# Sliding attention scores from 128 stacked rows: two full matmuls a block in place of three of 64 rows

## What is computed

```python
qb = q.reshape(b, nb, BLOCK, SWA_KV_HEADS, SWA_GROUP, SWA_HEAD_DIM)      # head size 64, blocks of 128 tokens
kk = jnp.concatenate([kp[:, :-1], kp[:, 1:]], axis=2)                    # the block before and the block itself
scores = jnp.einsum('bnqhgd,bnkhd->bnhgqk', qb, kk).astype(jnp.float32) * (SWA_HEAD_DIM ** -0.5)
scores = jnp.where(valid[None, :, None, None], scores + alibi, NEG)
probs = jax.nn.softmax(jnp.concatenate([scores, sink], axis=-1), axis=-1)[..., :-1]
out = jnp.einsum('bnhgqk,bnkhd->bnqhgd', probs.astype(v.dtype), vv)
```

## Time and profile before

| what | value |
|---|---|
| time, median of 3 runs | 2956.63 us (2955.93 to 2957.34) |
| span of the profiled execution, first to last instruction | 2956.8 us |
| PE busy | 2841.3 us, 96% of the span |
| DVE, ACT, POOL busy | 45%, 34%, 37% |
| mean granted TensorE clock | 0.975 |
| swa stages | about 160 to 410 us and 908 to 1160 us of the span |

### The profile page before, as it was taken

The page is one execution under the profiler, slowest core; times in us unless marked ns, Lnnn a source line. Parts: engine busy times, 40 slices in busy tenths (PEclk is TensorE's granted clock), DMA queues, the critical chain, the costliest instruction groups (busy, mean ns, idle before and its releaser), DMA issues.

```text
span 2956.8 us, 33732 instructions
## 1 busy us (share of the span) xinstructions
PE 2841.3 (96%) x13276; PEld 2324.0 (79%) x13276; DVE 1342.4 (45%) x1855; ACT 999.1 (34%) x1558; POOL 1092.7 (37%) x536
## 2 busy tenths in 40 slices
PE   7999999999999999999999999999999999999985
PEld 5888887778888888777777888788878888888774
DVE  6656545732365555474135445444344222222345
ACT  5234434522323343452333233323223232333221
POOL 3443341234443333222434333333434444444431
PEclk9999998999999999899999999999999999999997
DMA  5332231234433223113433222222323333336332
GB/s 158 105 102 72 72 113 37 55 100 139 139 93 121 72 68 117 42 42 96 137 123 85 72 72 75 75 72 68 97 86 112 110 114 107 114 107 214 110 111 93
DMA packets 307613, 288.11 MB, mean 97 GB/s; under 512 B 33152, under 2 KB 256000, under 8 KB 306944
## 3 DMA queue, kind: packets, MB, share of 16 engines
q1 hardware_dynamic: 300656, 263.93, 30.0%
q10 hardware_dynamic: 6800, 22.02, 1.9%
HBM read 259.66 MB, written 26.21 MB: 97 GB/s over the span
## 4 chain that ended last, share of the span: by engine, by line
PE 80%; DVE 13%; ACT 4%; issue 2%; POOL 1%; DMA 0%; DVEq 0%; SPq 0%; ACTq 0%
PE bank L813 23%; PE bank L815 22%; PE bank L814 22%; PE work L813 2%; DVE probs L1533 2%; PE work L814 1%; PE work L815 1%; PE o_bank L813 1%; PE work L1034 1%; PE o_bank L814 1%; PE o_bank L815 1%; DVE pt L1541 1%; DVE mixed L1109 1%; DVE mixed L1108 1%; POOL w_lo L804 1%
## 5 line engine op out<-in xcount | busy, mean ns | idle before, releaser
L804 POOL TENSOR_TENSOR w_lo<-w_raw,w_hi 128x1024 fp32r<-128x1024 f32 (+3 forms) x468 | 1004.0, 2148 | 1545.0 <-ACT w_hi L669 1544.8
L813 PE MATMUL bank<-act_in,w_hi 128*128 128x512 f32 x2664 | 1058.4, 397 | 38.4 <-DVEq L1194 24.7
L815 PE MATMUL bank<-act_in,w_lo 128*128 128x512 f32 x2664 | 1044.1, 392 | 0.0
L814 PE MATMUL bank<-act_in,w_hi 128*128 128x512 f32 x2664 | 1042.7, 391 | 0.0
L669 ACT ACTIVATE w_hi<-w_raw 128x1024 fp32r<-128x1024 f32 (+3 forms) x468 | 437.8, 937 | 1096.8 <-PE bank L815 700.3
L813 PEld LDWEIGHTS bank<-act_in,w_hi 128*128 128x128 f32 x2664 | 503.3, 189 | 149.4 <-POOL w_lo L804 18.3
L815 PEld LDWEIGHTS bank<-act_in,w_lo 128*128 128x128 f32 x2664 | 502.3, 189 | 108.2
L814 PEld LDWEIGHTS bank<-act_in,w_hi 128*128 128x128 f32 x2664 | 503.5, 189 | 99.3 <-issue 1.4
L813 PE MATMUL bank<-mixed,w_hi 128*128 128x512 f32 x768 | 303.0, 394 | 6.4 <-POOL w_lo L804 6.4
L814 PE MATMUL bank<-mixed,w_hi 128*128 128x512 f32 x768 | 301.7, 393 | 0.0
L815 PE MATMUL bank<-mixed,w_lo 128*128 128x512 f32 x768 | 301.0, 392 | 0.0
(11 more groups left out here) (230 smaller groups left out, 2897.7 us busy)
## 6 DMA issues: line engine op xcount, KB each, us to landing
w_raw<-in_w_in SPq DMA_DIRECT2D x512, 128.0 KB, 2.4
w_raw<-in_w_in SPq DMA_DIRECT2D x224, 256.0 KB, 2.9
w_raw<-in_w_out SPq DMA_DIRECT2D x64, 512.0 KB, 3.6
w_raw<-in_w_in SPq DMA_DIRECT2D x32, 512.0 KB, 3.7
w_raw<-in_w_out SPq DMA_DIRECT2D x64, 256.0 KB, 4.7
probs<-in_xT SPq DMA_DIRECT2D x32, 256.0 KB, 4.8
x_scr<-buf ACTq DMA_DIRECT2D x32, 256.0 KB, 2.2
probs<-x_scr SPq DMA_DIRECT2D x32, 256.0 KB, 4.9
```

What stands on the lines that cost most here:

```text
L804: nc.gpsimd.tensor_tensor(lo, raw, hi, ALU.subtract).then_inc(lo_ready, 1)
L813: pe.matmul(dst, lhs[0], rhs[0], start=start, stop=False, skip_group_check=skip)
L814: pe.matmul(dst, lhs[0], rhs[1], start=False, stop=False, skip_group_check=skip)
L815: return pe.matmul(dst, lhs[1], rhs[0], start=False, stop=stop, skip_group_check=skip)
```

## The change

The same query tile is held in another form. For each head e, `mixed[:, t, e]` now has all 128 partitions: the hi part of the head in its own 64 partitions and its lo part in the other 64. The keys get a plane pair for each e: `k_swa[:, e, 0]` has the keys' hi in both halves, `k_swa[:, e, 1]` has the keys' lo in the head's own half and zeros in the other. One matmul over 128 rows gives hi·hi + lo·hi, a second gives hi·lo, both with the same weights. The copies and subtractions on DVE are done by halves of 64 partitions, since a result has to go to the other half. `k_swa` has grown to 2048 columns and lies in another place, which the latents' DMA reads; so the keys are written in `swa_values`, behind the wait for that DMA.

```diff
-        k_swa = y_flat[:, 6144:7168].rearrange("p (s t) -> p s t", s=2)
+        k_swa = y_flat[:, 2048:4096].rearrange("p (e s t) -> p e s t", e=2, s=2)
...
-                    rows = slice(64 * e, 64 * e + 64)
...
-                        q = mixed[rows, t, :, i * P:(i + 1) * P]
-                        k = k_swa[rows, :, k0:k0 + w]
-                        ins = three(dst, (q[:, 0], q[:, 1]), (k[:, 0], k[:, 1]), True, True)
+                        q = mixed[:, t, e, i * P:(i + 1) * P]
+                        pe.matmul(dst, q, k_swa[:, e, 0, k0:k0 + w], start=True, stop=False)
+                        ins = pe.matmul(dst, q, k_swa[:, e, 1, k0:k0 + w], start=False, stop=True)
...
+            def head_rows(e):
+                return slice(64 * e, 64 * e + 64)
...
                     v.tensor_tensor(acc2[:, :], acc2[:, :], sq[:, :], ALU.add).then_inc(sum_in, 1)
-                    link(split(k_swa, tmp[:, 0, :]))
...
                 v.wait_ge(bank_free, tile_no[gi, m] + 1)
-                if m < 2:
-                    hi_lo = mixed[:, 2 * i + m] if kind == "swa" else (q_sb, k_sb[:, :, META:TM])[m]
-                    link(split(hi_lo, dst))
+                if kind == "swa":
+                    q = mixed[:, 2 * i + m]
+                    for e in range(2):
+                        ins = v.tensor_copy(q[head_rows(e), e, :], dst[head_rows(e), :])
+                    link(ins)
+                    for e in range(2):
+                        own, other = head_rows(e), head_rows(1 - e)
+                        ins = v.tensor_tensor(q[other, e, :], dst[own, :], q[own, e, :].bitcast(F32), ALU.subtract)
+                    link(ins)
+                elif m < 2:
+                    link(split((q_sb, k_sb[:, :, META:TM])[m], dst))
                 signal(tile_ready)
...
                     v.wait_ge(lat_saved, 16 * (l + 1))
+                    k = tmp[:, 0, :]
+                    for e in range(2):
+                        own, other = head_rows(e), head_rows(1 - e)
+                        v.memset(k_swa[other, e, 1, :].bitcast(F32), 0.0)
+                        v.tensor_copy(k_swa[other, e, 0, :], k[own, :])
+                        ins = v.tensor_copy(k_swa[own, e, 0, :], k[own, :])
+                    link(ins)
+                    for e in range(2):
+                        own = head_rows(e)
+                        v.tensor_tensor(k_swa[own, e, 1, :], k[own, :], k_swa[own, e, 0, :].bitcast(F32),
+                                        ALU.subtract)
```

## The result

The changed kernel takes **2972.27 us** (median of 4 runs, 2968.74 to 2977.13) against 2956.28 us before: a ratio of **1.0051, 95% interval 1.0037 to 1.0065**. Measured once more later, with more rounds, it was 1.0069 (1.0053 to 1.0084). It is slower, by 11 to 25 us. The profiled execution is the fastest of the four: its span is 2967.0 us, and the run's time 2968.74.

What follows compares the result with a forecast made beforehand. DVE with ACT was taken to bound the swa group ends, with PE waiting; 2956.8 less 19.5 gained on PE plus 34 lost gives 2971.3, forecast 2971 us, range 2955 to 2984.

Steps and rivals of the forecast that it cites:

- The bound: At the 8 swa group ends DVE with ACT is the bound; PE waits 0.4 us before the first head's transposes.
- The gain: PE's score blocks: 0.83 us a head, 19.5 us in sum; the 8 first heads bring nothing.
- a part for the form: PE's score blocks: leaving matmuls of 64 rows gives back 0.38 us a head.
- one for the number: PE's score blocks: four matmuls fewer a head give 0.45 us.
- The loss: DVE's added query splits at the 8 group ends, with standing behind POOL: 34 us in sum.
- A group end of the usual kind: Six group ends: 4.2 us more each, 2.3 of work and 1.9 behind POOL; 25.2 us.
- a layer's first group end: First group end of each layer: 4.5 us each, 9 us for two; bounds 1.7 and 7.
- POOL: DVE's copies and subtractions at a group end stand 1.9 us behind POOL's instructions.
- The rival in which POOL is missed: Group ends: additions cost only 1.15 us a read; about 2954 us, 2962 with half the collisions; chance 0.15.
- The clock: TensorE's clock falls at group ends: taken as 0, since PE's second wait absorbs it; upper end 13.6 us.
- a second wait of 2 us before the first heads' transposes: At a group end PE, after standing some 3 us before a product, waits some 2 us more until L1493 is done.
- The keys: Key split in `swa_values`, 4.1 us a layer on DVE: costs nothing, or up to 1.5 us a layer behind POOL.

Runs made afterwards that it cites:

- DVE's halves: Kernel before, with only the query tiles split in halves of 64 partitions (two copies, two subtractions): 2992.85 us, 1.0127 of before.
- q1 later in the kernel before: Kernel before, with q1's copy and subtraction moved behind the request for the first head's exponentials: 2950.18 us, 0.9982 of before.
- PE's form alone: Changed kernel with its two 128-row matmuls and key work, but query tiles split on DVE as before: 2942.42 us, again 2941.06 us (0.9943 of before).
- the experiment without its pair: Changed kernel with POOL's subtraction cut to one column per row for one chunk per swa group end: 2959.98 us, 1.0013 of before.

## Why the prediction was right

- **The bound.** That PE waits for DVE at a group's end was right (experiments with DVE's halves and with q1 later in the kernel before). The prediction says that the trace before shows this wait at each of the 8 ends; it shows it at seven. At the first end of the second layer the transposes start at 922.58 without idle time, and the second head's scores follow the first's after 12.16 us, not 13.04.
- **The gain.** 0.83 us a head against 0.86 in the trace; 19.5 us in sum against 17.4 us of the stages. The split in a part for the form (24 x 0.38 = 9.1 us) and one for the number (24 x 0.45 = 10.8) came out as 8.4 and 9.0. Most of the missing 2 us sits at a place that the prediction had free of waits, the second head of a layer's last group. PE, DVE and POOL there, after:

```profile
378.13 0.98 PE L1033 MATMUL work<-ident,probs 128*128 128x128 f32 x7 [0.19 <-DVEq L1196]
382.60 0.33 PE L964 MATMUL work<-mixed 128*128 128x128 f32 x1 [0.72 <-DVE pt L1561]
```

```profile
378.17 3.18 DVE L1423 TENSOR_TENSOR buf<-buf 128x1024 f32<-128x1024 f32 x1
```

```profile
377.82 2.45 POOL L804 TENSOR_TENSOR w_lo<-w_raw,w_hi 128x1024 fp32r<-128x1024 f32 x1 [3.74 <-ACT w_hi L669]
```

In the kernel before, this DVE instruction (there L1414) started 0.29 us ahead of POOL and took 1.23 us; now it starts 0.35 us behind POOL and takes 3.18, and L1561, which PE wants for the third head's scores, comes after it. From the second head's scores to the third's it is 382.60 - 368.48 = 14.12 us, where the group before has 12.83. That is 1.3 us once in each layer, 2.6 in sum, and it is in the profiles of PE's form alone as well. 17.4 + 2.6 = 20.0 us is about what 24 heads of 0.83 us give, 19.9.
- **The loss.** 34 us against 32.7 of the stages. A group end of the usual kind: 4.2 against 4.01. For a layer's first group end 4.5 was taken. In the profile after, L1496 comes 11.76 us after the read of q0 begins in the first layer and 9.64 us in the second (from 910.86), where L1476 came 6.32 us after it: +5.4 and +3.3 us.

```profile
159.05 0.69 DVE L1324 TENSOR_TENSOR buf<-bank,r_x 128x512 f32<-128x512 f32 x1 [0.42 <-PE bank L815]
...
170.81 0.55 DVE L1496 SCALAR_TENSOR_TENSOR probs<-delta,work 128x384 f32<-128x384 f32 x1 [0.34 <-DVE buf L1208]
...
920.50 0.56 DVE L1496 SCALAR_TENSOR_TENSOR probs<-delta,work 128x384 f32<-128x384 f32 x1 [0.34 <-DVE buf L1208]
```

In the first layer the split of q1 meets two pairs of POOL. In the second profile of the changed kernel both ends take 11.7 to 11.8 us. So 4.5 lies between what the cases cost.
- **POOL.** 1.9 us at a group end against 1.7 on DVE (the experiment without its pair). The rival in which POOL is missed fell.
- **The clock.** In the profile after it fell from 2.4 to 1.2 GHz at all eight group ends, with 17 us at the low level in each swa stage: at seven of them during or right behind the wait for L1208, at the first end of the second layer only behind a wait of 1.90 us for the transposes; the first wait was 1.04 us there. A fall between the two waits was absorbed as described. I had forecast a second wait of 2 us before the first heads' transposes; in the changed kernel PE idles only 0.26 us there at this group end. The windows between the two waits tell why. After:

```profile
294.50:302.20 7.70, 7.37 (x25) 5.57 (x25) 4.82 (x11) 4.00 (x12) 0.72 (x1) 0.78 0.11 30
```

and without POOL's pair, where PE's first wait was 1.26 us and the clock stayed at its high level:

```profile
293.40:301.10 7.70, 5.75 (x25) 4.45 (x25) 4.80 (x11) 4.02 (x12) 0.74 (x1) 1.00 0.04 10
...
301.08 1.18 PE L1038 MATMUL work<-ident,probs 128*128 128x128 f32 x6 [1.89 <-DVEq L1201]
```

With a grant of 1.00 the second wait is there, 1.89 us; with 0.78 (0.22 x 2 x 7.7 = 3.4 us at the low level, 1.7 us lost) it is gone. So this one step was told wrong in size for the likeliest case, and right in the sum. The profile of DVE's halves alone has both cases in one kernel, from the first head's scores to the second's at the second end of each layer:

```profile
230.34:247.40 17.06, 14.29 (x62) 11.03 (x61) 11.07 (x19) 7.14 (x16) 5.72 (x4) 0.90 0.15 40
988.72:1005.76 17.04, 12.73 (x62) 9.84 (x61) 11.06 (x19) 7.13 (x16) 5.72 (x4) 1.00 0.15 39
```

With the fall (3.4 us at the low level behind the wait for L1206) PE waits 0.32 us for the transposes, without it 1.89 us, and the stretch is equally long. The forecast's other half came true too: "only a fall after the second costs". At the third end of the second layer the second profile of the changed kernel (first row) has the fall behind the wait for the transposes, the first profile (second row) behind the wait for L1208. DVE needs 11.39 us from the read of q0 to L1208 in both:

```profile
1046.82:1065.05 18.23, 13.39 (x58) 10.54 (x57) 12.14 (x19) 7.18 (x17) 5.71 (x4) 0.91 0.19 51
```

```profile
1040.11:1057.25 17.14, 13.60 (x58) 10.36 (x57) 11.04 (x19) 7.19 (x17) 5.72 (x4) 0.90 0.14 39
```

The late fall costs 1.1 us. The first end of that layer is 2.1 us longer in the second profile, since two pairs of POOL stand in DVE's way there instead of one (10.16 us to L1208 against 8.02). These two ends make up nearly all of the 3.3 us between the profiles.

- **The keys** cost nothing (measured), but it was close: in the changed kernel DVE has 0.42 us left before the read of q0 (at 159.05 above) where it had 5.19.

The sum 2971 is near the 2972.27 also by luck: the gain was taken 2.1 us too high and the loss 1.3 us, and the second measurement of the same kernel gave 2975.92.

## What to carry to other kernels

A matmul saved is worth its pace only where PE is waited for: follow the timeline of each engine from a bank's read to the next step that PE needs, and see whether any idle time stands in it. An engine with 45% load can bind at a few places, and there every instruction that a new layout needs counts in full, plus what it runs into on another engine. What DVE gives back is not yet what PE gets back: without POOL's pair DVE was 1.7 us earlier, and PE gained 0.6 us where the clock fell late. The cure was to move work that is wanted late into the engine's own wait for an answer, and to issue the instruction that somebody waits for a few tenths of a us before the other engine begins.

## What the runs showed of the hardware

- Blocks of 64-row matmuls between blocks of 128 rows cost 0.38 us each time beyond their number: twelve in 2.25 us from product to product, against 1.86 with 128 rows.
- Who starts first on DVE and POOL decides: the same scaling of 768 columns on DVE took 2.06 us when it started 0.03 us behind POOL's instruction, and 0.96 us when it started 0.36 us ahead of it, while POOL's went from 1.27 to 1.75 us.
- A fall of TensorE's clock for 3.4 us cost nothing where PE had another wait of 1.9 us ahead (17.06 against 17.04 us), and 1.1 us where it came behind PE's last long wait (18.23 against 17.14 us).
